# Hybrid attention and GLA block on eight cores: GLA keys and gated outputs transposed by DMA instead of by TensorE

## What is computed

```python
proj = rmsnorm(x) @ w_in        # aq ak av gq gk gv g_lr g_r gate_a gate_b, 12816 columns
A = sliding_window_attention(aq, ak, av)            # 32 query heads of 64, 4 KV heads, window 128, sinks
G = gla(gq, gk, gv, log_sigmoid(g_lr @ w2 + b)/16)  # 4 heads, keys 256 wide, values 512 wide
G = rmsnorm_per_head(G) * silu(g_r)
h = x + (sigmoid(gate_a) * A + sigmoid(gate_b) * G) @ w_out
out = rmsnorm(h + (silu(v2 @ w_gate) * (v2 @ w_up)) @ w_down)   # v2 = rmsnorm(h), hidden width 5632
```

## Time and profile before

| | us |
|---|---|
| median of 3 runs (3782.21 to 3783.95) | 3782.68 |
| the profiled execution | 3786.89 |
| span of its slowest core, core 5 | 3785.3 |
| spans of the eight cores | 3775.6 to 3785.3 |
| PE busy on core 5 | 3695.9 (98%) |
| DVE, ACT, POOL busy | 1200.2, 964.9, 755.6 |
| granted TensorE clock, mean of core 5 | 0.993 |

### The profile page before, as it was taken

How to read it: one execution, slowest core, us unless ns; L and a number is a source line. 1 busy time by engine, 2 the same in 40 slices (tenths; PEclk the granted TensorE clock), 3 DMA queues, 4 the chain that set the end, 5 groups by cost and what they waited for, 6 DMA issues and landing times.

```text
span 3785.3 us, 50247 instructions; the slowest of 8 cores (3775.6 to 3785.3 us)
## 1 busy us (share of the span) xinstructions
PE 3695.9 (98%) x18688; PEld 1717.2 (45%) x18688; DVE 1200.2 (32%) x1919; ACT 964.9 (25%) x2028; POOL 755.6 (20%) x756
## 2 busy tenths in 40 slices
PE   5999999999999999999999999999999999999998
PEld 3444444444444444444444444444444444444443
DVE  4677534422311011111127774434223111100003
ACT  2455433423200000011125544433241000000000
POOL 2233333432100000000003323334311010100000
PEclk8999999999999999999999999999999999999999
DMA  9535375449965656378683443565399777763566
GB/s 135 79 49 70 39 95 79 55 74 169 162 90 75 81 68 88 61 125 151 118 122 55 61 65 48 81 95 84 53 212 142 112 124 129 108 81 65 117 118 161
DMA packets 426416, 368.84 MB, mean 97 GB/s; under 512 B 13728, under 2 KB 378272, under 8 KB 426048
## 3 DMA queue, kind: packets, MB, share of 16 engines
q0 software_dynamic: 373856, 268.58, 53.3%
q1 hardware_dynamic: 52320, 97.06, 9.6%
HBM read 586.78 MB, written 47.38 MB: 168 GB/s over the span
## 4 chain that ended last, share of the span: by engine, by line
PE 90%; DMA 4%; DVE 3%; issue 2%; ACT 1%; POOL 0%; SPq 0%; DVEq 0%; ACTq 0%; POOLq 0%
PE ps L368 79%; PE psS L368 8%; DMA hd<-hw 2%; DMA xn<-x 1%; PE ps L705 1%; PE psS L506 1%; ACT a_P L373 0%; DVE gl L766 0%; DMA out<-hsl 0%; DVE a_sel L667 0%; ACT gl L373 0%; DVE gm L376 0%; DVE a_sm L670 0%; DVE a_sd L688 0%; ACT L373 0%
## 5 line engine op out<-in xcount | busy, mean ns | idle before, releaser
L368 PE MATMUL ps<-X,wsl 128*128 128x512 bf16 x8832 | 1943.2, 380 | 2.6 <-DVE X L376 2.6
L368 PEld LDWEIGHTS ps<-X,wsl 128*128 128x128 bf16 x8832 | 853.5, 98 | 1044.5 <-issue 45.0
L368 PE MATMUL ps<-wsl,X 128*128 128x512 bf16 (+1 forms) x3328 | 723.8, 373 | 0.6 <-DMA wsl<-w_in 0.6
L368 PEld LDWEIGHTS ps<-wsl,X 128*128 128x128 bf16 x3328 | 323.3, 98 | 350.5 <-issue 1.6
L376 DVE TENSOR_TENSOR ffT<-ps,silu 128x512 bf16<-128x512 f32 x176 | 121.7, 692 | 1051.3 <-PE ps L368 1051.3
L373 ACT ACTIVATE silu<-ps 128x512 bf16<-128x512 f32 x176 | 105.1, 597 | 1101.8 <-PE ps L368 1101.8
L368 PE MATMUL ps<-wsl,ffT 128*128 128x512 bf16 x1716 | 379.2, 379 | 1.0 <-DVE ffT L376 1.0
L368 PEld LDWEIGHTS ps<-wsl,ffT 128*128 128x128 bf16 x1716 | 167.0, 98 | 199.0 <-issue 1.5
L368 PE MATMUL psS<-wsl,ffT 128*128 128x512 bf16 x1100 | 244.8, 379 | 0.0
L349 POOL DMA_DIRECT2D wsl<-w_g x44 | 51.3, 1165 | 954.7 <-PE ps L368 954.4
L368 PE MATMUL ps<-wsl,mT 128*128 128x512 bf16 x1024 | 227.0, 381 | 2.1 <-DVE hw L376 2.1
(11 more groups left out here) (164 smaller groups left out, 2506.9 us busy)
## 6 DMA issues: line engine op xcount, KB each, us to landing
wsl<-w_in POOLq DMA_DIRECT2D x40, 2048.0 KB, 19.5
wsl<-w_g POOLq DMA_DIRECT2D x44, 1024.0 KB, 11.6
wsl<-w_u POOLq DMA_DIRECT2D x44, 1024.0 KB, 15.8
wsl<-w_d POOLq DMA_DIRECT2D x16, 1920.0 KB, 15.4
hsl<-hd SPq DMA_DIRECT2D x96, 256.0 KB, 6.6
wsl<-w_in POOLq DMA_DIRECT2D x20, 1024.0 KB, 15.3
hw<-x SPq DMA_DIRECT2D x64, 256.0 KB, 10.3
wsl<-w_out POOLq DMA_DIRECT2D x8, 2048.0 KB, 27.4
```

Source lines behind the costliest of these rows:

```text
L368: ins = e.matmul(o_, lhsT=l_, rhs=r_, start=s0, stop=s1)
```

## The change

The keys are transposed by DMA: right after DVE has written the 512 tokens of one half of the key dimension, SP issues one transposing DMA of 128 x 512 into `g_ktok`, which now holds all eight tiles of a head and lies at another place (it overlaps `hw` 4 to 6). c1 loses its two PE transposes and ACT's copy. The gated output is transposed by one DMA of 128 x 512 per tile, which writes into the `g_rs` buffer that the tile no longer needs; c3 is now DVE's add alone. All 96 transposing DMAs (32 for keys, 64 for outputs) are issued by SP in its one order. c3(b) is no longer recorded as a step of its own pair but kept in `late`, and recorded after the next c1(a), or at g = 0, t = 6 of the output projection. In `wout_stage` the loads for steps 6, 7 and 8 are recorded together in step 4 (before: in steps 2, 3 and 4).

```diff
--- before.py
+++ after.py
@@ -283,7 +283,7 @@
     g_tmp = [alloc("g_tmp", [512], F32, at=c + (20 + 2 * j) * KB) for j in range(2)]
     g_S2 = [alloc("g_S2", [512], F32, at=c + (24 + 2 * j) * KB) for j in range(2)]
     g_G = [alloc("g_G", [512], BF16, at=c + (28 + j) * KB) for j in range(2)]
-    g_ktok = [alloc("g_ktok", [256], BF16, at=c + 30 * KB + 512 * j) for j in range(2)]
+    g_ktok = alloc("g_ktok", [NTL, 256], BF16, at=c + 68 * KB)
     g_attm = [alloc("g_attm", [128], BF16, at=c + 31 * KB + 256 * j) for j in range(2)]
     g_sc = [alloc("g_sc", [3, 2, 8], F32, at=M0 + 75 * KB + 256 * j) for j in range(2)]
     qd = alloc("qd", [2, HT], BF16, at=M0 + 40 * KB)
@@ -746,6 +746,15 @@
 
 
     gbank = ["s"]
+    late = []
+
+    def flush():
+        while late:
+            late.pop(0)()
+
+    def xbar(out_ap, in_ap, reads, writes, chan):
+        S.op("sp", lambda e: e.dma_start_transpose(out=out_ap, in_=in_ap), reads=reads, writes=writes, dma=True,
+             chan=("xb",) + chan)
 
     def gates_pre(h, tb):
         for dk in range(2):
@@ -818,22 +827,11 @@
                [("ps", b)])
             am = g_attm[t % 2]
             tt("dve", am.ap, ps[b][:, 0:128], tri.ap, ALU.mult, [("ps", b), "tri"], am.all)
-            b2 = bank("s")
-            tv = trview(b2)
-
-            def tr(e):
-                ins = None
-                for dk in range(2):
-                    ins = e.transpose(out=tv[:, dk, :], in_=ki.ap[:, dk, cs], identity=identb.ap)
-                return ins
-            S.op("pe", tr, reads=kk + ["identb"], writes=[("ps", b2)])
-            kt = g_ktok[t % 2]
-            copy("act", kt.ap, tv[:, 0:2, :].rearrange("p a b -> p (a b)"), [("ps", b2)], kt.all)
 
         def c2(t):
             tb = t // 4
             cs = slice(t * 128, (t + 1) * 128)
-            am, kt, v = g_attm[t % 2], g_ktok[t % 2], g_v[t % 4]
+            am, v = g_attm[t % 2], g_v[t % 4]
             bo = bank("s")
             first = half * NTL + t == 0
             l = [(ps[bo][:, :], am.ap, v.ap, True, first)]
@@ -852,30 +850,24 @@
             for dk in range(2):
                 bu = bank("s")
                 bus.append(bu)
-                mm([(ps[bu][:, :], kt.ap[:, dk * 128:(dk + 1) * 128], v.ap, True, True)], kt.all + v.all, [("ps", bu)])
+                mm([(ps[bu][:, :], g_ktok.ap[:, t, dk * 128:(dk + 1) * 128], v.ap, True, True)],
+                   g_ktok.k(t, t + 1, dk * 128, (dk + 1) * 128) + v.all, [("ps", bu)])
                 s2 = g_S2[dk]
                 stt(st_.ap[:, dk, :], ps[bu][:, :], sc.ap[:, 1, dk, t:t + 1], s2.ap, ALU.mult, ALU.add,
                     [("ps", bu), ("gsc", h % 2, 1, tb)] + s2.all, st_.k(dk, dk + 1))
             rs = g_rs[t % 4]
             stt(G.ap, ps[bo][:, :], r, rs.ap, ALU.mult, ALU.mult, [("ps", bo)] + rk + rs.all, G.all)
+            xbar(rs.ap.rearrange("p (a b) -> p a b", a=4), G.ap, G.all, rs.all, ("G", t % 4))
 
         def c3(t):
-            G = g_G[t % 2]
-            b = bank("s")
-            tv = trview(b)
-
-            def tr(e):
-                ins = None
-                for j in range(4):
-                    ins = e.transpose(out=tv[:, j, :], in_=G.ap[:, j * 128:(j + 1) * 128], identity=identb.ap)
-                return ins
-            S.op("pe", tr, reads=G.all + ["identb"], writes=[("ps", b)])
+            gt = g_rs[t % 4]
             mk_ = mT.k(h * 4, h * 4 + 4, t * 128, (t + 1) * 128)
             mv = mT.ap[:, h * 4:(h + 1) * 4, t * 128:(t + 1) * 128]
-            tt("dve", mv, tv, mv, ALU.add, [("ps", b)] + mk_, mk_)
+            tt("dve", mv, gt.ap.rearrange("p (a b) -> p a b", a=4), mv, ALU.add, gt.all + mk_, mk_)
 
         a, b_ = t0, t0 + 1
         c1(a)
+        flush()
         yield
         c2(a)
         yield
@@ -885,7 +877,7 @@
         yield
         c3(a)
         yield
-        c3(b_)
+        late.append(lambda: c3(b_))
         if t0 == NTL - 2 and half == 0 and h < 3:
             spdma(sd[h], st_.flat, st_.all, [("sd", h)], ("ss", h % 2))
         yield
@@ -904,6 +896,9 @@
                     tt("dve", ki.ap[:, dk, tb * 512:(tb + 1) * 512], ps[b][:, :], ei.ap[:, dk, :], ALU.mult,
                        [("ps", b)] + ei.k(dk, dk + 1), ki.k(dk, dk + 1, tb * 512, (tb + 1) * 512))
                 grp_feat(slot, 256 + dk * 128, 128, tb, evk)
+                xbar(g_ktok.ap[:, tb * 4:tb * 4 + 4, dk * 128:(dk + 1) * 128], ki.ap[:, dk, tb * 512:(tb + 1) * 512],
+                     ki.k(dk, dk + 1, tb * 512, (tb + 1) * 512),
+                     g_ktok.k(tb * 4, tb * 4 + 4, dk * 128, (dk + 1) * 128), ("k", tb, dk))
                 if tb == 1 and dk == 1:
                     issue_load()
                 tick()
@@ -1001,12 +996,16 @@
                 slot = take()
             if g == 0 and t == 6:
                 drain(chain_q)
+                flush()
             b = bank("m")
             mm([(ps[b][:, :], mT.ap[:, k, t * 128:(t + 1) * 128], wsl[slot].ap[:, k, :], k == 0, k == KC - 1)
                 for k in range(KC)], wres(slot) + mT.k(0, KC, t * 128, (t + 1) * 128), [("ps", b)])
             if t == NTL - 1:
                 issue_load()
-            if i >= 2:
+            if i == 4:
+                for q in (6, 7, 8):
+                    xload(q)
+            elif i > 4:
                 xload(i + 4)
             hs = hw[i % 8]
             tt("dve", hs.ap, ps[b][:, :], hs.ap, ALU.add, [("ps", b)] + hs.all, hs.all)
```

## The result

The change makes the kernel slower. The ratio of after to before is 1.0033, with a 95% interval of 1.0018 to 1.0048; the medians are 3783.2 us before (12 of 16 executions) and 3795.5 us after (11 of 16). The profiled execution took 3799.52 us, with a span of 3798.0 us on core 1 (before: 3785.3 on core 5).

What follows compares the result with a forecast made beforehand. PE, busy 98% of the span and never idle in GLA, was taken as the bound. Terms -21.1 + 1 + 5.5 + 1.5 = -13.1 us took 3782.7 to 3769.6 us; range 3758 to 3796.

Steps and rivals of the forecast that it cites:

- rival B: In GLA, transposing DMAs take longer than 17 us while weights stream and PE stands: 3796 to 3861 us; chance 0.20.
- PE's transposes: In GLA, removing 384 transposes from a PE that never idles there saves 21.1 us.
- Rows 5: Profile rows of the chain in GLA: 0.22 us for a c3's four transposes, 0.11 for a c1's two, 55 ns each.
- rival C: In GLA, transposes hold PE longer than the chain says, 42.3 us by busy time: 3748 us; chance 0.04.
- The transposing DMA: In GLA, output transposes land in 10.4 us, bounds 6.7 and 20.8; DVE waits at times, PE never: cost 0.
- threshold of 17 us: In GLA, PE stalls only if a transposing DMA takes over 17 us: 10 us of room plus 7 from banks.
- The first x load: At the output projection's start, loads 0 to 5 queue behind tile 5's transpose: 0.5 us per half, 1 in all.
- Load 6: In the output projection, it waits for tile 7's transpose and comes 3 us late, covered by two free banks.
- The store of step 3: In the output projection, it leaves 5.5 us later behind tile 7's transpose and loads, starting a chain; 5.5 us, once.
- The 1.5 us for traffic: In the output projection's saturated stretch, two more output transposes and early x lengthen six hops: 1.5 us.
- Rival A: The output projection gives it all back, 20.5 against 21.1 us, through chain, hops and first load: 3782 us; chance 0.16.
- D: In GLA, PE's transposes go but DMA or DVE sets the pace, so the span stays: 3782 us; chance 0.03.

Runs made afterwards that it cites:

- f12: Repeat of e6 (after with x loads 0 to 3 early, head 3's tiles 6 and 7 transposed by PE, store ahead of load); ratio to before 0.9920, median 3761.9 us.
- f9: The kernel before, with each step's store in the output projection recorded ahead of the next load; ratio to before 0.9973, median 3784.0 us.
- f10: The changed kernel, with each step's store in the output projection recorded ahead of the next load; ratio to before 0.9995, median 3788.2 us.
- e2: The changed kernel, but the gated outputs of head 3's tiles 6 and 7 transposed by PE and merged at the old step; ratio to before 1.0116.
- e3: The changed kernel with x loads 0 to 3 ahead of head 3's rounds and head 3's tiles 6 and 7 transposed by PE; ratio to before 0.9965.
- e4: The kernel before, with only the loads for steps 6, 7 and 8 recorded together in step 4; ratio to before 1.0023.
- e6: e3 with each step's store in the output projection recorded ahead of the next load; ratio to before 0.9927.
- e5: The kernel before, with the first six x loads held until tile 5's gated output of head 3 is ready; ratio to before 1.0011.

## Why the prediction was wrong

I forecast 3769.6 us and faster; it was slower by 0.33%. The sign is wrong, and 0.20 of chance stood on slower, for another reason than the true one. That 3795.5 us lies inside my range (to 3796) is luck: I had set that end by rival B, which did not happen.

**PE's transposes: right.** 21.1 us was forecast; the starts of the projections moved by 19.8 us and f12 against f9 gives 22. Rows 5 were the right price. For 368 transposes (16 stay on PE) 22 us is 60 ns each. The Trainium skill, TensorE: Matmul & The Clock Gate (Part 4), has about 275 ns in a kernel's context; a rival by that figure would have been five times too large, and busy time (rival C) twice.

**The transposing DMA: right, better than thought.** I took 10.4 us and allowed 20.8. The page's tile view of `g_G` in after and the DMA view (count, median) have

```profile
DMA to landing us min/median/max: 2.4/5.9/14.4
```

```profile
g_rs<-g_G SPq DMA_TRANSPOSE x64, 5.9
g_ktok<-ki SPq DMA_TRANSPOSE x32, 8.5
```

It never reached my threshold of 17 us, so rival B had no ground. In 400 to 850, most of GLA, DVE waits 5.6 us in all:

```profile
DVE mT L376 <- DMA g_rs<-g_G: 5.6, 6, 1.2
```

The Trainium skill, VectorE: DVE Perf Modes (The three transpose paths), gave an estimate of 5.2 us for 128 x 512. Its estimate lies between the least and the median here.

**The threshold of 17 us: the step that failed.** "PE rotates over three banks, so it feels nothing for two more groups" holds where PE's next group depends on DVE by its bank only. At the end of head 3 it doesn't: the merge of tile 7 is the group's *input*. I put 0 for it, and it cost 5.7 us of idle PE in the first half (4 to 5 on f10's cores) and a restart at the lower clock. I had the transposes' latency, the merge's place and step 7, and never asked who reads `mT` first. There no bank helps; the room is the time from G to the merge's reader. From G's end at 885.2 to the end of the merge at 897.63 it took 12.4 us of queue, flight and add, 5.7 more than PE had. The Trainium skill, VectorE: DVE Perf Modes (Rules for kernel authors), prefers TensorE for a 128 x 128 transpose where a PSUM result is fine; these runs agree for the last two tiles of a half (e2, e3) and not for the other thirty.

**The first x load: mechanism right, size wrong.** I had it go 7.7 us ahead of DVE's wish, 0, 2.7 or 10.4 us late, and 3 us of slack behind it, so 0.5 per half. It went 861.83 - 855.46 = 6.4 us ahead and was 5.0 us late, inside my bounds. The slack was the error: I let only the mask stand behind DVE's add and left out ACT's two passes over `hw` ahead of `Sbf`. PE stood 4.99 us for 5.0 of lateness, so there was none. In place of 1 us for both halves, this stall and the other together cost 27 us in f10.

**Load 6: not decided.** I costed it at 0. e4 shows no longer projection from it, but a mean core that is 3 to 5 us slower.

**The store of step 3: place right, size wrong.** I took 5.5 us once, as the second half had room. That store itself left about as forecast. On after's core 1 the add of step 3 ends at 881.17 and the store goes at 888.13, 7.0 us later; before, on core 5, it went 0.1 us after the add, so it is 6.9 us late by this count:

```profile
884.38 0.69 DVE L376 TENSOR_TENSOR hw<-ps,hw 128x512 f32<-128x512 f32 x1 [2.79 <-PE ps L368]
```

But what followed was 0 to 18 us on the first half and 0 to 13 on the second, above f10's 130.5, and it is a chain by the order of recording, since e6, f9 and f10 end it. The 1.5 us for traffic stays open: f12 takes 117.0 us, but no transpose falls into its projections, and in f10 the two stalls hide so small a term.

**Rival A was the nearest** and had 0.16. Its place (the output projection gives it back) is right; I priced it mostly with hops of the chain, 20.5 us in all, while 27 us came from the two stalls, one of which it didn't have, and the chain came on top. **D** is false: in 600 to 700 PE is at 100.00.

The balance: with the stores first the change costs 4.2 us by the medians of f9 and f10, 5 on the mean core and 8 by the ratios, against 27 - 22 = 5 from the terms. The rest of the 12 us is the longer chain of after, less before's own: 8 us by the medians, 4 by the ratios. So stalls less gain and the chain each have a share of 4 to 8 us, and which is the larger isn't settled.

## What to carry to other kernels

A transfer that replaces an engine's step is hidden only up to the first reader of its result; free banks cover a late evacuation and not a late operand, so look at the last tile before the consumer and leave it to the engine if need be. On one issuing queue, ask for each moved DMA what was recorded behind it, and for each waiter all the followers on every engine down to the one that bounds. Issue stores that release buffers ahead of the loads that wait for them.

## What the runs showed of the hardware

- A transposing DMA of 128 x 512 bf16 from SBUF to SBUF (the 64 of gated outputs, after) landed in 2.4 us at least, 5.9 median, 14.4 at most; the median is unsteady, 2.6 in e3. A transpose made 544 packets on the mean, nearly all under 512 B, and kept SP busy for 1.2 us or more (1.18, 1.44, 1.70) where an x load took some 0.5 (3.31 for six).
- The first x load of 256 KB, issued right behind such a transpose, reached DVE's add 11.4 us after its issue in the median of after's cores, and 8.7 us in e5, where no DMA transposes. Whether the transpose ahead of it or something else is the reason, no run separates.
- In the window of 5 us in which PE resumed after a stall of some 5 us, its granted clock was 0.50 to 0.73 (after, f10), and a stall cost about 1.4 us beyond its idle time, an estimate from f10 (13.5 - 10.7, over two).
